# Two-layer hybrid decoder step: the sample recurrence with the state as moving operand, and a rearranged opening

## The chip, the cores and the metric

One NeuronCore of one Trainium2 chip runs one program: two layers of a hybrid decoder. The metric is device time in microseconds (us) of that one execution; every figure below is in microseconds unless it says otherwise.

## What is computed

A layer normalises its input, projects it once to all branches, runs three token mixers and merges them. There are 256 prompt tokens and 8 sample sequences of 8 tokens (64 tokens), 320 tokens in all; the model width is 2048.

```python
h = rms_norm(x, norm_g)
proj = h @ w_in                       # all branch inputs and the merge gates
...
# branch C, gated linear attention, 4 heads, dk 128, dv 256, per sequence:
o = einsum('bhtd,bhde->bhte', qi * exp(b), S)                  # the state read
att = einsum('bhtd,bhsd,bhtsd->bhts', qi, ki, decay)
o = o + einsum('bhts,bhse->bhte', att, vi)
S = exp(b_last)[..., None] * S + einsum('bhsd,bhse->bhde', ki * exp(b_last - b), vi)
...
y = x + merged @ w_out
```

The eight sample sequences start from a state `S` each (4 heads of 128 x 256), and the new states are outputs. The change concerns the line "the state read" for the sample sequences, and the very beginning of the first layer: the scaled input `x * norm_g` and the sum of squares that the norm needs.

## The kernel before, in words

All activations lie transposed: channels on partitions, the 320 tokens along the free axis. Weights stream from HBM in pieces of 128 x 1024 fp32 (512 KB), 298 for each layer. The work on one piece is called a **beat**. For exactness every operand is split into a high part that TensorE takes in its fp32r form and a low part, the rest: ScalarE writes `w_hi` (`split_hi`), VectorE writes `w_lo` (`split_lo`), in two halves of 512 columns, two beats ahead. A beat on TensorE is then 24 matmuls of 128 x 128 weights on 320 tokens (`block_products`: hi x hi, hi x lo, lo x hi), in two halves with a semaphore each.

A layer has 122 beats of input projection, 144 of gates and branch projections and 32 of output projection. Between the beats of the first stretch stand the small matmuls of the mixers, the **side steps**. A hand-written table (`side_steps`, `put(beat, name, k, banks)`) says after which beat each is issued, and which banks of the PSUM tensor `side` it uses. Each engine runs its own program in the order of the beats: in beat b VectorE and ScalarE first split the weights of beat b+2 and then do what the step of beat b hands them (`vector_part`, `scalar_part`). `free_banks` makes TensorE wait until the last reader of a bank has read it.

**The sample recurrence** is eight side steps `sample_gla`, after beats 53, 55, ... 67. Step k takes one head h and one half of the sample sequences (four sequences). For each of two 128-wide pieces of dv it multiplies `att_s` with `v_gla` (64 x 128 weights, 32 columns), and for each of four sequences b a 128 x 128 piece of the sequence's state as weights with eight query columns of `lev_q` (128 x 8), in fp32. The sums stand in bank 3 of `side`, dv on partitions, and after step 7 ScalarE copies all of it into `o_c` (line 1093). Then four fp32r matmuls of 256 columns (`v_stack`, `k_sel`) give the state's increment; VectorE adds it to the decayed state (`sample_state`, line 646) and prepares the next step's `k_sel` (`sample_sel`, line 624). GpSimd's queue (POOL) loads and stores the states, three buffers in turn.

An fp32 matmul of the program stands in the trace as two records; an fp32r one as one.

**The opening** (layer 0, beats 0 to 3): ScalarE's queue issues `params` and the eight pairs of 128-row pieces of x (320 KB each), SyncE's queue (SP) the weight pieces, POOL's queue the constants, masks and the first small weights (2.5 MB). For each pair ScalarE writes `xg_hi` (line 989) and the square of x (line 992), VectorE `xg_lo` (line 415) and two additions to `sq_sum` (lines 419, 423). TensorE needs pairs 0 and 1 and the first weight piece for beat 0, pairs 2 and 3 for beat 1, and so on. After beat 3 it sums `sq_sum` over partitions with one matmul, and ScalarE makes the inverse root of it (`inverse_root`, lines 979, 981, with a table load at line 950). VectorE turns a mask into bytes and clears `q_s` in beat 5 (lines 776, 777); POOL's next loads and two copies from HBM to HBM wait for that.

## Time and profile before

| | us |
|---|---|
| median of 3 runs | 2437.93 (2436.49 to 2440.85) |
| the profiled execution | 2442.46 |
| its span from the first to the last instruction | 2440.7 |
| TensorE (PE) busy | 2382.1, 98% of the span |
| VectorE (DVE) busy | 1374.5, 56% |
| ScalarE (ACT) busy | 1012.4, 41% |
| mean granted TensorE clock | 0.983 of full speed |
| bytes moved | 360.68 MB, 148 GB/s on average |

PE is busy nearly all the time, and the chain of work that ended last lies on it for 87% of the span. So the time is made of what PE is given to do, of the few places where it waits, and of the clock that it is granted. A record of a matmul carries its start and its modelled end; matmuls overlap, so what a matmul costs is read from the distance between starts, not from the duration. The timeline joins neighbouring records of one kind (xN), and gives the start of the first and the length to the end of the last.

### The profile page before, as it was taken

To read this page: it belongs to the slowest core of one execution; us is meant where nothing else is said; L and a number is where in the kernel's file an instruction comes from. 1 tells how busy PE (TensorE), PEld (TensorE's weight loads), DVE (VectorE), ACT (ScalarE), POOL (GpSimd) and SP (SyncE) were. 2 spreads that over 40 slices of the span, in tenths; PEclk is the share of its full clock that TensorE was granted. 3 is DMA by queue.
4 is the path that set the end of the run, shared out by engine and by line. 5 is a ranking of instruction groups with operands and counts; after the bars stand their busy time and mean duration, and the time that the engine had idled before them with its cause. 6 is when DMAs were issued, how large, how long until landed. Compare 5 with 4: busy or idle time off the path is not lost.

```text
span 2440.7 us, 38676 instructions
## 1 busy us (share of the span) xinstructions
PE 2382.1 (98%) x16192; PEld 2334.3 (96%) x16192; DVE 1374.5 (56%) x2324; ACT 1012.4 (41%) x1813; POOL 71.9 (3%) x110
## 2 busy tenths in 40 slices
PE   6999999899999999999999999998999999999998
PEld 6999999799999999999999999998999999999998
DVE  5666656665545455546656675666555455554443
ACT  5335345654333333333342442456443333333332
POOL 0010000000000000000000100000000000000000
PEclk9999999999999999999999998999999999999999
DMA  6333554223444444445553434532244444444453
GB/s 256 113 112 131 187 194 136 90 93 117 152 147 152 151 147 151 152 147 189 195 203 104 147 131 171 189 121 94 80 138 148 153 149 148 153 149 148 153 201 121
DMA packets 97134, 360.68 MB, mean 148 GB/s; under 512 B 11376, under 2 KB 11376, under 8 KB 96128
## 3 DMA queue, kind: packets, MB, share of 16 engines
q1 hardware_dynamic: 85824, 312.51, 38.6%
q0 software_dynamic: 9840, 43.02, 4.8%
q8 instruction: 128, 2.10, 0.4%
q10 hardware_dynamic: 1296, 2.67, 0.3%
q14 instruction: 46, 0.38, 0.1%
HBM read 341.59 MB, written 20.50 MB: 148 GB/s over the span
## 4 chain that ended last, share of the span: by engine, by line
PE 87%; DVE 6%; ACT 3%; issue 2%; DMA 1%; ACTq 0%; POOL 0%; DVEq 0%; POOLq 0%
PE main L1382 79%; PE side L1382 8%; DVE w_lo L380 2%; ACT w_hi L961 1%; ACT probs L1118 1%; PE side L1386 1%; DMA x_first<-in_x_pairs 1%; ACT tc L1158 1%; DVE small L698 0%; DVE probs L693 0%; DVE ta L395 0%; DVE cb L544 0%; DVE probs L721 0%; DVE xg_lo L415 0%; DVE lev_e L558 0%
## 5 line engine op out<-in xcount | busy, mean ns | idle before, releaser
L1382 PE MATMUL main<-xg_hi,w_hi 128*128 128x320 f32 x3488 | 1105.4, 317 | 22.8 <-DVE w_lo L380 20.5
L380 DVE TENSOR_TENSOR w_lo<-raw,w_hi 128x512 fp32r<-128x512 f32 x1192 | 794.3, 700 | 538.7 <-ACT w_hi L961 527.5
L1382 PE MATMUL main<-xg_lo,w_hi 128*128 128x320 f32 x3488 | 1088.1, 312 | 0.0
L1382 PE MATMUL main<-xg_hi,w_lo 128*128 128x320 f32 x3488 | 1087.6, 312 | 0.0
L961 ACT ACTIVATE w_hi<-raw 128x512 fp32r<-128x512 f32 x1192 | 715.8, 627 | 711.3 <-PE main L1382 698.5
L1382 PEld LDWEIGHTS main<-xg_hi,w_hi 128*128 128x128 f32 x3488 | 665.3, 191 | 33.9 <-DVE sq_sum L423 16.7
L1382 PEld LDWEIGHTS main<-xg_lo,w_hi 128*128 128x128 f32 x3488 | 665.3, 191 | 2.0
L1382 PEld LDWEIGHTS main<-xg_hi,w_lo 128*128 128x128 f32 x3488 | 664.2, 190 | 0.0
L1382 PE MATMUL main<-branch_hi,w_hi 128*128 128x320 f32 x768 | 237.3, 309 | 0.0
L1382 PE MATMUL main<-branch_lo,w_hi 128*128 128x320 f32 x768 | 237.3, 309 | 0.0
L1382 PE MATMUL main<-branch_hi,w_lo 128*128 128x320 f32 x768 | 237.3, 309 | 0.0
L1382 PE MATMUL main<-mg_hi,w_hi 128*128 128x320 f32 x512 | 158.2, 309 | 0.0
L1382 PE MATMUL main<-mg_lo,w_hi 128*128 128x320 f32 x512 | 158.2, 309 | 0.0
L1382 PE MATMUL main<-mg_hi,w_lo 128*128 128x320 f32 x512 | 158.2, 309 | 0.0
L1382 PEld LDWEIGHTS main<-branch_hi,w_hi 128*128 128x128 f32 x768 | 144.1, 188 | 0.0
L1382 PEld LDWEIGHTS main<-branch_lo,w_hi 128*128 128x128 f32 x768 | 144.1, 188 | 0.0
L1382 PEld LDWEIGHTS main<-branch_hi,w_lo 128*128 128x128 f32 x768 | 144.1, 188 | 0.0
L1216 ACT ACTIVATE tb<-ta 128x640 f32<-128x640 f32 x48 | 35.6, 742 | 179.8 <-DVE ta L866 179.8
L866 DVE TENSOR_TENSOR ta<-main,rstd 128x640 f32<-128x640 f32 x48 | 39.6, 825 | 103.8 <-PE main L1382 103.8
L1382 PEld LDWEIGHTS main<-mg_hi,w_hi 128*128 128x128 f32 x512 | 96.1, 188 | 0.0
L1382 PEld LDWEIGHTS main<-mg_lo,w_hi 128*128 128x128 f32 x512 | 96.1, 188 | 0.0
L1382 PEld LDWEIGHTS main<-mg_hi,w_lo 128*128 128x128 f32 x512 | 96.1, 188 | 0.0
(218 smaller groups left out, 1459.2 us busy)
## 6 DMA issues: line engine op xcount, KB each, us to landing
raw<-in_w_stream SPq DMA_DIRECT2D x596, 512.0 KB, 3.3
state<-in_state POOLq DMA_DIRECT2D x16, 512.0 KB, 6.2
out_state_s<-state POOLq DMA_DIRECT2D x16, 512.0 KB, 3.0
x_first<-in_x_pairs ACTq DMA_DIRECT2D x8, 320.0 KB, 16.3
w_pool<-in_w_pool POOLq DMA_DIRECT2D x2, 1024.0 KB, 10.7
cache_k<-in_cache_k POOLq DMA_DIRECT2D x2, 1024.0 KB, 5.8
cache_v<-in_cache_v POOLq DMA_DIRECT2D x2, 1024.0 KB, 8.9
out_k_window<-in_cache_k_tok POOLq DMA_DIRECT2D x2, 960.0 KB, 9.9
```

What stands on the lines that cost most here:

```text
L380: dve.tensor_tensor(w_lo[Q % RAWS][:, half], raw[Q % RAWS][:, half], w_hi[Q % HIS][:, half].bitcast(F32), ALU.subtract).then_inc(lo_ready, 1)
L866: dve.tensor_tensor(ta[:, :, :], group_psum(G0), two(rstd[:, :]), ALU.mult).then_inc(main_free, 1)
L961: act.activation(w_hi[Q % HIS][:, half], raw[Q % RAWS][:, half], ACT.Copy).then_inc(hi_ready, 1)
L1118: a(act.activation(p[:, lo:lo + n], p[:, lo:lo + n], ACT.Exp, bias=small[:, 4 + i:5 + i], accum_out=small[:, 12 + i:13 + i]))
L1158: ins = act.activation(tc[32 * q:32 * q + 32, :, :], ta[32 * (q ^ 1):32 * (q ^ 1) + 32, :, :], ACT.Copy)
L1216: give(act.activation(tb[:, :, :], ta[:, :, :], ACT.Sigmoid))
L1382: return pe.matmul(out, lhsT, rhs, start=start, stop=stop)
L1386: return pe.transpose(out, src, ident[0:src.shape[0], 0:src.shape[0]])
```

## The change

Two independent edits stand in one kernel.

**Sample recurrence.** Steps now go half by half (k = 4 * half + head) and not head by head. The state becomes the moving operand: for each of four sequences a matmul with 32 weight columns from the new tile `q_pad` (queries of one head in their own eight columns, zeros beside them) and the 256 columns of the sequence's state. The four write to partitions 0, 32, 64 and 96 of `side` bank 3, and accumulate over the four heads. After the last head of a half ScalarE copies the result, tokens on partitions, to `o_tok`. A new side step `sample_out` (after beat 67, bank 2) adds `att_s` times `v_gla` (8 matmuls of 64 columns) and turns `o_tok` to dv on partitions with a permuted identity (4 matmuls of 128 columns). The steps stand after beats 53, 55, 57, 59, 61, 63, 65, 66. VectorE fills `q_pad` twice in a layer (`sample_queries`, beats 50 and 59).

**Opening.** The odd pairs of x go on SP's queue, between the weight pieces; POOL's loads wait until beat 3 is done. ScalarE loads its table at the start. The squares, 640 columns at a time into `sq_part`, come in beats 1 to 3, after all x has been split; VectorE adds them in whole pairs. The norm's matmul moves from beat 3 to beat 4 (both layers), the first `take` from beat 3 to beat 5, the masks from beat 5 to beat 10.

```diff
+SAMPLE_AT = (53, 55, 57, 59, 61, 63, 65, 66)
...
     for k in range(8):
-        put(53 + 2 * k, "sample_gla", k, (0, 1, 3))
+        put(SAMPLE_AT[k], "sample_gla", k, (0, 1, 3))
+    put(67, "sample_out", 0, (2,))
...
+TAKE[0] = 5
+RMS_BEAT = 4
+def x_at(beat):
+    return {0: (4, 5), 1: (6, 7)}.get(beat, ())
+def squares_at(beat):
+    return {1: (0, 1), 2: (2, 3, 4), 3: (5, 6, 7)}.get(beat, ())
...
             def first_x(j):
-                from_act()
-                sq = (tb, tc)[j % 2]
+                dve.wait_ge(x_hi_ready, j + 1)
...
-                if j == 0:
-                    v(dve.tensor_tensor(sq_sum[:, :], sq[:, 0, :], sq[:, 1, :], ALU.add))
-                else:
-                    for t in range(2):
-                        v.settle()
-                        v(dve.tensor_tensor(sq_sum[:, :], sq_sum[:, :], sq[:, t, :], ALU.add))
+            def first_squares(j):
+                from_act()
+                if j:
+                    tt(sq_part[:, :, :], sq_part[:, :, :], (tb, tc)[j % 2][:, :, :], ALU.add)
                 v.mark("squares_added", 0, j)
+                if j == 7:
+                    tt(sq_sum[:, :], sq_part[:, 0, :], sq_part[:, 1, :], ALU.add)
...
+            def sample_queries(l, half):
+                if half:
+                    wait_step(l, "sample_gla", GH - 1)
+                else:
+                    v(dve.memset(q_pad[:, :], 0.0))
+                    v.settle()
...
+                for h in range(GH):
+                    v(dve.tensor_copy(dst[:, h], src[:, h]))
...
-                if l == 0 and beat == 5:
+                if l == 0 and beat == 10:
                     dve.wait_ge(consts_in, 64)
                     v(dve.tensor_copy(gmask[:, :, :], gmask_f[:, :, :]))
...
-            for j in range(8):
+            for j in (0, 2, 4, 6):
                 act.dma_start(x_first[:, 2 * j:2 * j + 2, :], ins["x_pairs"][j]).then_inc(x_in[j], 16)
+            use_ln_exp()
...
-                    elif name == "sample_gla" and k == 7:
+                    elif name == "sample_gla" and k % GH == GH - 1:
+                        half = k // GH
                         wait_step(l, name, k)
-                        a(act.activation(o_c[:, :, SEQ:TOK], side[:, 3, :].rearrange("p (c n) -> p c n", c=8), ACT.Copy))
+                        a(act.activation(o_tok[:, half, :], side[:, 3, 256 * half:256 * half + 256], ACT.Copy))
+                        a.mark("sample_tok", l, half)
+                    elif name == "sample_out":
+                        wait_step(l, name, k)
+                        a(act.activation(o_c[:, :, SEQ:TOK], side[:, 2, :].rearrange("p (c n) -> p c n", c=8), ACT.Copy))
...
                 sp.dma_start(raw[Q % RAWS][:, :], ins["w_stream"][Q]).then_inc(raw_in[Q % RAWS], 16)
+                if Q < 4:
+                    sp.dma_start(x_first[:, 4 * Q + 2:4 * Q + 4, :], ins["x_pairs"][2 * Q + 1]).then_inc(x_in[2 * Q + 1], 16)
...
+            pool.wait_ge(half_used, last_half(0, 3))
+            load(w_gate[0:RANK, :], ins["w_gate"][0], w_gate_in)
             load(const[:, :], ins["consts"], consts_in)
...
                 elif name == "sample_gla":
-                    h, half = divmod(k, 2)
+                    half, h = half_head(k)
                     pe.wait_ge(state_in[k % STATES], 16 * state_load(l, k))
                     wm("k_sel", l, k)
-                    for t in range(2):
-                        c = 2 * h + t
-                        n = 32 * half
-                        mm(side[:, 3, SMP * c + n:SMP * c + n + 32], v_gla[0:SMP, 2, P * c:P * c + P],
-                           att_s[0:SMP, SMP * h + n:SMP * h + n + 32], True, False)
-                        for b in range(4):
-                            n = 32 * half + TS * b
-                            mm(side[:, 3, SMP * c + n:SMP * c + n + TS], state[:, k % STATES, b, P * t:P * t + P],
-                               lev_q[:, h, SEQ + n:SEQ + n + TS], False, b == 3)
+                    if h == 0:
+                        wm("queries", l, half)
+                    for b in range(4):
+                        mm(side[32 * b:32 * b + 32, 3, 256 * half:256 * half + 256],
+                           q_pad[:, P * h + 32 * b:P * h + 32 * b + 32], state[:, k % STATES, b, :],
+                           h == 0, h == GH - 1)
                     for b in range(4):
                         last = mm(side[:, b // 2, 256 * (b % 2):256 * (b % 2) + 256], k_sel[0:96, b, :],
                                   v_stack[half][0:96, DV * h:DV * h + DV])
+                elif name == "sample_out":
+                    wm("sample_tok", l, 1)
+                    for c in range(8):
+                        pe.matmul(side[:, 2, SMP * c:SMP * c + SMP], v_gla[0:SMP, 2, P * c:P * c + P],
+                                  att_s[0:SMP, SMP * (c // 2):SMP * (c // 2) + SMP], start=c == 0, stop=False,
+                                  skip_group_check=True)
+                    pick = ident.rearrange("p (j h t) -> p h j t", j=4, h=GH)
+                    o4 = side[:, 2, :].rearrange("p (h c n) -> p h c n", h=GH, c=2)
+                    for half in range(2):
+                        for c in range(2):
+                            out = o4[:, :, c, 32 * half:32 * half + 32].rearrange("p h (j t) -> p h j t", j=4)
+                            last = pe.matmul(out, o_tok[:, half, P * c:P * c + P], pick, start=False, stop=True,
+                                             skip_group_check=True)
...
-                    if beat == 3:
+                    if beat == RMS_BEAT:
                         wait_mark(pe, "sq_sum", l, 0)
```

Below is the order of the instructions at three places. The first is the first sample step on TensorE, after the last matmuls of beat 53; `main` is the projection, `side` the step. Before:

```order
L1382 MATMUL main<-xg_hi,w_lo_67 128x320
L1382 MATMUL side<-att_s,v_gla 128x32
L1382 MATMUL side<-lev_q,state 128x8 x4
L1382 MATMUL side<-att_s,v_gla 128x32
L1382 MATMUL side<-lev_q,state 128x8 x4
L1382 MATMUL side<-v_stack_112,k_sel 128x256 x4
L1382 MATMUL main<-xg_hi,w_hi_69 128x320
```

The same place on TensorE in the changed kernel, where `q_pad` gives the 32 weight columns:

```order
L1454 MATMUL main<-xg_lo,w_hi_71 128x320
L1454 MATMUL main<-xg_hi,w_lo_67 128x320
L1454 MATMUL side<-state,q_pad 32x256 x4
L1454 MATMUL side<-v_stack_114,k_sel 128x256 x4
L1454 MATMUL main<-xg_hi,w_hi_69 128x320
```

Ten matmuls with 8 or 32 moving columns have become four with 256; the four of the state's increment are as they were.

The second place is ScalarE's program at the start, with what each row waits for; `tb` and `tc` hold the squares. Before:

```order
L970 DMA par<-in_params 128x98
L972 DMA x_first<-in_x_pairs 128x640 x8
L989 ACT_TABLE_LOAD [waits x_in0,params_in]
L989 ACTIVATE xg_hi<-x_first,par 128x320 [waits vec_done]
L989 ACTIVATE xg_hi<-x_first,par 128x320
L992 ACTIVATE tb<-x_first 128x640
L989 ACTIVATE xg_hi<-x_first,par 128x320 [waits x_in1]
L989 ACTIVATE xg_hi<-x_first,par 128x320
L992 ACTIVATE tc<-x_first 128x640
L961 ACTIVATE w_hi_69<-raw_59 128x512 [waits raw_in0]
```

The same start of ScalarE's program in the changed kernel:

```order
L1024 DMA x_first<-in_x_pairs 128x640 x4
L1002 ACT_TABLE_LOAD
L1040 ACTIVATE xg_hi<-x_first,par 128x320 [waits x_in0,params_in,vec_done]
L1041 ACTIVATE xg_hi<-x_first,par 128x320
L1040 ACTIVATE xg_hi<-x_first,par 128x320 [waits x_in1]
L1041 ACTIVATE xg_hi<-x_first,par 128x320
L1013 ACTIVATE w_hi_69<-raw_59 128x512 [waits raw_in0]
```

The table load no longer stands behind the first x, and the two squares have left the way to the first `w_hi`.

The third place is VectorE's program up to the first `w_lo`, before:

```order
L415 SCALAR_TENSOR_TENSOR xg_lo<-x_first,par,xg_hi 128x320 [waits act_given,params_in,vec_done]
L415 SCALAR_TENSOR_TENSOR xg_lo<-x_first,par,xg_hi 128x320
L419 TENSOR_TENSOR sq_sum<-tb 128x320
L415 SCALAR_TENSOR_TENSOR xg_lo<-x_first,par,xg_hi 128x320 [waits act_given]
L415 SCALAR_TENSOR_TENSOR xg_lo<-x_first,par,xg_hi 128x320
L423 TENSOR_TENSOR sq_sum<-sq_sum,tc 128x320 [waits vec_done] x2
L380 TENSOR_TENSOR w_lo_64<-raw_59,w_hi_69 128x512 [waits hi_ready] x2
```

The same stretch of VectorE's program in the changed kernel:

```order
L448 SCALAR_TENSOR_TENSOR xg_lo<-x_first,par,xg_hi 128x320 [waits x_hi_ready,params_in,vec_done]
L448 SCALAR_TENSOR_TENSOR xg_lo<-x_first,par,xg_hi 128x320
L448 SCALAR_TENSOR_TENSOR xg_lo<-x_first,par,xg_hi 128x320 [waits x_hi_ready]
L448 SCALAR_TENSOR_TENSOR xg_lo<-x_first,par,xg_hi 128x320
L414 TENSOR_TENSOR w_lo_64<-raw_59,w_hi_69 128x512 [waits hi_ready] x2
```

The additions of squares have left, and `xg_lo` waits for `xg_hi` alone.

## Rows read from the trace of the kernel before

**Rows 1.** The page: PE's busy time; the projection's first product, busy and idle.

```profile
PE 2382.1 (98%) x16192; PEld 2334.3 (96%) x16192; DVE 1374.5 (56%) x2324; ACT 1012.4 (41%) x1813; POOL 71.9 (3%) x110
...
L1382 PE MATMUL main<-xg_hi,w_hi 128*128 128x320 f32 x3488 | 1105.4, 317 | 22.8 <-DVE w_lo L380 20.5
```

**Rows 2.** Timeline of PE, first sample step: start, length, instruction, tile, shape.

```profile
263.20 0.31 PE L1382 MATMUL main<-xg_hi,w_lo 128*128 128x320 f32 x1
263.44 0.40 PE L1382 MATMUL side<-att_s,v_gla 64*128 64x32 f32 x2
263.78 1.06 PE L1382 MATMUL side<-lev_q,state 128*128 128x8 f32 x8
...
266.01 0.72 PE L1382 MATMUL side<-v_stack,k_sel 96*128 96x256 f32 x4
266.57 0.31 PE L1382 MATMUL main<-xg_hi,w_hi 128*128 128x320 f32 x1
...
273.71 0.41 PE L1382 MATMUL side<-att_s,v_gla 64*128 64x32 f32 x2
```

**Rows 3.** Stretches: from:to, length, busy (x) by engine, granted clock, DMA share, GB/s.

```profile
294.20:306.00 11.80, 11.80 (x73) 11.50 (x72) 6.62 (x12) 2.48 (x5) 1.06 (x2) 0.86 0.61 215
...
263.40:345.60 82.20, 82.20 (x557) 80.00 (x557) 50.06 (x87) 25.11 (x42) 6.90 (x13) 0.96 0.51 177
1464.00:1550.00 86.00, 86.00 (x563) 83.64 (x562) 49.81 (x87) 24.59 (x41) 6.89 (x13) 0.92 0.48 166
```

**Rows 4.** Timeline of PE, steps whose matmuls write to two partition halves in turn.

```profile
413.51 1.14 PE L1382 MATMUL side<-probs,v_tok 128*64 128x128 f32 x12
414.58 0.41 PE L1382 MATMUL main<-xg_hi,w_hi 128*128 128x320 f32 x1
...
512.19 0.45 PE L1382 MATMUL side<-cache_k,q_s 128*64 128x128 f32 x4
```

**Rows 5.** Timeline of PE, fp32 matmuls of 256 moving columns in the second chunk.

```profile
229.16 1.89 PE L1382 MATMUL side<-v_gla,ko_tok 128*128 128x256 f32 x8
```

**Rows 6.** Timeline of all engines, the opening up to the first matmul.

```profile
1.17 4.27 ACTq L972 DMA_DIRECT2D x_first<-in_x_pairs  x8
...
7.77 1.28 ACT L989 ACT_TABLE_LOAD   x1 [7.77 <-DMA x_first<-in_x_pairs]
...
9.99 0.72 ACT L992 ACTIVATE tb<-x_first 128x640 f32<-128x640 f32 x1
...
11.31 1.02 ACT L989 ACTIVATE xg_hi<-x_first,par 128x320 fp32r<-128x320 f32 x2 [0.61 <-DMA x_first<-in_x_pairs]
...
12.87 1.13 ACT L961 ACTIVATE w_hi<-raw 128x512 fp32r<-128x512 f32 x2
12.99 1.01 DVE L415 SCALAR_TENSOR_TENSOR xg_lo<-x_first,par,xg_hi 128x320 fp32r<-128x320 f32 x2 [0.72 <-ACT tc L992]
...
14.98 1.28 DVE L380 TENSOR_TENSOR w_lo<-raw,w_hi 128x512 fp32r<-128x512 f32 x2
...
15.81 0.61 PE L1382 MATMUL main<-xg_hi,w_hi 128*128 128x320 f32 x1 [15.81 <-DVE w_lo L380]
```

**Rows 7.** Timeline of PE, first matmuls of beats 1 to 3, and the norm's.

```profile
23.03 0.38 PE L1382 MATMUL main<-xg_hi,w_hi 128*128 128x320 f32 x1 [0.73 <-DVE w_lo L380]
...
27.69 0.38 PE L1382 MATMUL main<-xg_hi,w_hi 128*128 128x320 f32 x1 [0.90 <-DVE xg_lo L415]
...
32.84 0.39 PE L1382 MATMUL main<-xg_hi,w_hi 128*128 128x320 f32 x1 [1.41 <-DVE xg_lo L415]
...
36.44 0.70 PE L1382 MATMUL side<-sq_sum,ones 128*128 128x320 f32 x2
```

**Rows 8.** DMA of the first 22 us: all packets, and POOL's queue (q0).

```profile
DMA packets 2559, 7.79 MB, mean 354 GB/s; under 512 B 447, under 2 KB 447, under 8 KB 2431
...
q0 software_dynamic: 544, 2.49, 28.1%
```

**Rows 9.** Timeline of DVE in beat 10, waiting for the gate step.

```profile
64.17 1.93 DVE L534 TENSOR_SCALAR lev_q<-side,par 128x320 f32<-128x320 f32 x4 [3.35 <-PE side L1382]
```

More of the change, by code:

```diff
@@ L258, in trunk @@
         probs = [probs0, probs1]
+        q_pad = place("q_pad", [P, GH * (P + TS)], at=probs0_at)
         main = ctx.enter_context(nc.psum_tensor("main", [P, 4, 512], F32))
@@ L766, in vector_part @@
             def vector_part(l, beat):
-                if l == 0 and beat < 2:
-                    for j in range(4 + 2 * beat, 6 + 2 * beat):
-                        first_x(j)
-                if l == 0 and beat == 1:
-                    v.settle()
-                    v.mark("sq_sum", 0, 0)
-                if l == 0 and beat == 5:
+                if l == 0:
+                    for j in squares_at(beat):
+                        first_squares(j)
+                if l == 0 and beat == 10:
                     dve.wait_ge(consts_in, 64)
@@ L848, in vector_part @@
                 for k in range(8):
-                    if beat == 51 + 2 * k:
+                    if beat == (SAMPLE_AT[k - 1] if k else 51):
                         sample_sel(l, k)
+                if beat in (50, SAMPLE_AT[GH - 1]):
+                    sample_queries(l, int(beat != 50))
                 if beat in (68, 70):
@@ L917, in _ @@
                         split_lo(1)
+                    if l == 0:
+                        for j in x_at(beat):
+                            first_x(j)
                     vector_probs(l, beat)
@@ L1040, in scalar_part @@
             def scalar_part(l, beat):
-                if l == 0 and beat < 2:
-                    for j in range(4 + 2 * beat, 6 + 2 * beat):
-                        first_x(j)
-                if beat == 3:
+                if l == 0:
+                    for j in squares_at(beat):
+                        first_squares(j)
+                if beat == RMS_BEAT:
                     act.wait_ge(rms_done, l + 1)
@@ L1227, in _ @@
                         split_hi(1)
+                    if l == 0:
+                        for j in x_at(beat):
+                            first_x(j)
                     split_hi(Q + 2)
@@ L1294, in _ @@
                 for k in range(STATES):
-                    load(state[:, k, :, :], ins["state"][l, k], state_in[k])
+                    load(state[:, k, :, :], ins["state"][l, state_no(k)], state_in[k])
                 s, n = marks[("hist", l, 3)]
```

45 lines of the change are left out of this document (32 added, 13 removed).

## The prediction

> **What bounds the kernel now.** I read the page first: TensorE (PE) is busy 98% of the span, and the projection's largest group waited only 22.8 us in all, of which 20.5 on `w_lo` [rows 1]. So there are three things to gain from: matmul time, the few waits, and the clock. The timeline of PE then gives the prices, always from start to start. A projection matmul takes 0.147: the last of beat 53 starts at 263.20, so the next would start at 263.35. The next projection matmul starts at 266.57 [rows 2]; a sample step therefore costs 3.22, sixteen times, 51.5. The next step starts 10.27 later: 24 matmuls at 0.147 are 3.52, and two such beats and one step make 10.26, so PE has no wait here.
>
> The clock comes next. The stretch of one such period from 294.20 to 306.00 lasts 11.80 and not 10.27, at a mean granted clock of 0.86 [rows 3]; TensorE has two levels, 1.2 and 2.4 GHz, and it fell to the lower one right behind a step. Over the whole phase the mean is 0.96 in layer 0 and 0.92 in layer 1 [rows 3]. Time times the missing share is 3.3 and 6.9; with 1.53 for each spoilt period, two in layer 0, it is 3.1, and so I take 3.1 and 6.1, together 9.2.
>
> The opening: the first matmul starts at 15.81 [rows 6]; beats 1, 2 and 3 then begin with waits of 0.73, 0.90 and 1.41, and the norm's matmul comes at 36.44 [rows 7].
>
> **The sample step.** Removed are two `att_s` matmuls and eight of the state with eight columns: everything from 263.35 to 266.01, 2.66, most of it paid for loading 128 weight columns for eight moving ones (eight records in 1.06, or 0.115 each) [rows 2]. Added are four fp32 matmuls of 256 columns. Such a matmul is two records of 0.216: eight records take 1.89 including a last duration of about 0.38 [rows 5]. One after the other the four would take 1.73. Side by side, each in its own 32 columns of the array, they would take 0.43. What does the trace say of that? In the attention step with two halves of 64 columns, twelve records of 128 columns, half as many as in [rows 5] and so 0.108 each, take 1.07 from the first start to the next projection matmul at 414.58 [rows 4]; in a row they would be 1.30, in perfect parallel 0.65. Four records at 512.19 end within 0.45, less than the 0.60 of a row of four at 0.108 with a last duration of 0.27 [rows 4]. So two column tiles do overlap, with a loss of 0.2 to 0.42 at the seams. Four tiles at a time no row shows. The bounds are 0.43 and 1.73 plus the change of tile shape, 0.09 on each side (a first side matmul comes 0.24 behind the projection and not 0.147 [rows 2]). I take full overlap with a loss of 0.3: 0.09 + 0.43 + 0.30, and the unchanged four `k_sel` matmuls, 0.12 each, 0.48 [rows 2]. That is **1.30 a step**, a gain of 1.92, sixteen times **30.7**. The lower bound (no loss but the tile change) is 1.09 (34.1), the serial one 2.39 (13.3).
>
> The Trainium skill speaks against the overlap, in "TensorE: Matmul & The Clock Gate", Part 3 (Packing small matmuls): a weight load passes an in-flight matmul only when its row group differs, and column tiles share the row groups. By that rule the four would come one after the other; the two-half steps of this trace do not agree. The same part gives 2.38 times for three column tiles, which would put the four, as an estimate with the same efficiency for each tile, near 0.55 and the sum 2.9 lower.
>
> **The new step `sample_out`.** Eight fp32 matmuls of 64 columns with 64 x 128 weights are sixteen records at 0.115 to 0.13 (like the `att_s` pair, 0.40 less one duration of 0.27, and the eight-column row) [rows 2]: 1.84 to 2.1. Four of 128 columns are eight records at 0.115: 0.92. With the changes of shape this is 3.0, twice: **6.0** added. It waits for ScalarE's copy of step 7's output, a PSUM read of 256 columns. Beat 67, 3.52, lies between, and ScalarE's queue holds nothing else there but a copy for the gate; I cost the wait at nothing, and at 1 if the cover is gone.
>
> **Waits in the shorter phase.** Two beats and a step now last 8.34 and not 10.27. VectorE is busy 50.06 of 82.20 [rows 3]; the same work in 66 is three quarters, with the splits still two beats ahead. I place its work in a period: take, state, `k_sel`, two splits, two products, and each `w_lo` is ready 3 or more before PE wants it. `k_sel` for step 7 is the tightest, as steps 6 and 7 are now one beat apart: VectorE needs about 0.3 + 1.7 + 0.7 behind step 6, against 3.52. The state for step 7 is loaded behind step 5, which leaves some 11 for a store issue, a load issue and a landing. The fills of `q_pad` (a memset and four small copies) stand on VectorE's queue behind the pooling's work; queued behind them is a `w_lo` two beats ahead. Nothing for all of this, up to 1 if one is late.
>
> **The clock.** Removed are the long stretches of almost empty matmuls behind which it fell. I give back all **9.2**; none is the other bound, and then the new `sample_out` (2 us of narrow matmuls, where a step had 2.7) is where it would fall.
>
> **The opening.** DMA moved 7.79 MB in the first 22 us, of it 2.49 by POOL's queue [rows 8]. Without those and with two queues for x, I expect pair 0 at 6.4 (it was 7.77) and pair 1 at 6.2 (it was 11.31) [rows 6]. The table load of 1.28, which stood behind pair 0, is under the wait. From there: two pairs of `xg_hi` at 1.02, a `w_hi` piece of 1.13; VectorE's `xg_lo` at 1.01 a pair ends at 9.5 and the first half of `w_lo` (half of 1.28) at 10.1 [rows 6]. So PE starts at **10.1**, 5.7 earlier; the squares (0.72 each) and additions that stood between are moved. Bounds are 9.3 and 12: x slower than I count.
>
> Do beats 1 to 3 still wait? On ScalarE each beat needs 2.04 of `xg_hi` and 1.13 of `w_hi`, 3.2; on VectorE 2.02 and 1.28, 3.3, below 3.52, and PE's first beat gives time as well: before it took from 15.81 to 22.30 (23.03 less its wait), 2.97 over the 3.52, at the lower clock (its first record is 0.61 long, later ones 0.31 [rows 2, 6, 7]). I take 2.5 for that after. x and the first five weight pieces are the 5.3 MB that are left of the 7.79 [rows 8]; at the same 0.4 MB/us they are in by 16.5, pair 7, just ahead of the last piece, at 15.2. Counting both engines on from there, its `xg_lo` ends at 19.3, and PE wants it at 23.1 (10.1 + 3 x 3.52 + 2.5). So the three waits, 3.0, go too. PE is through beat 3 at 26.7 (10.1 + 14.1 + 2.5) against 36.44: **9.7**. What is late next is the norm: squares of pairs 5 to 7 end on ScalarE near 27, their additions on VectorE near 28.5, and PE asks after beat 4, at 30.1. Masks in beat 10 (1.6) fall into VectorE's 3.35 of waiting for the gate step [rows 9]. Constants are issued at 27 and wanted at about 50. The HBM copies now run in beats 11 and 12 and delay weight pieces there, which are a beat or more ahead.
>
> **Sum.** 30.7 - 6.0 + 9.2 + 9.7 = 43.6. From the profiled execution's 2442.46 (span 2440.7 and 1.8 around it) this gives 2398.9; that execution stands 4.5 above the median of the runs, 2437.93, from which it gives 2394.3. The runs differ by how often the clock falls, which the 9.2 was read from at the high end. I forecast the middle, **2396**; the rivals are counted from the same middle, 2440.2.
>
> **Rivals.**
> Tiles in a row: the four matmuls don't overlap, by the rule named above or another. A step is 2.39, the gain 13.3 and not 30.7, and the clock may still fall behind it (half of 9.2): 2440.2 - 13.3 + 6.0 - 4.6 - 9.7, about 2419. For it: no row with four tiles. Against: [rows 4]. 0.12.
> Two at a time: the moving operands of four tiles can't all be read at once. Four records' time, 0.86, and the loss: a step of 1.73, gain 23.8: 2403. 0.15.
> The clock falls elsewhere: steps and opening as forecast, but low stretches stand behind `sample_out` or in the attention, whose waits now fall otherwise: 2405. 0.10.
> Slower than before: a wide moving operand of fp32 state in a 32-column tile runs at a quarter of its rate, in a row. The four then take 6.9, a step 7.6; sixteen times 4.3 is 69, less 9.7 and plus 6.0: about 2505. It decides from a step of 3.5 on, where 16 times the excess over 3.22 eats the opening's net 3.7. For it: no row moves fp32 through so narrow a tile. Against it: the `v_tok` step keeps its rate in tiles of 64 columns [rows 4]. 0.02.
> The opening does not do what it says: x is no earlier because weights and x share the bandwidth, and only the table load and squares (1.28 + 1.44) are saved: 2403. 0.06, else as forecast.
>
> **How the numbers follow.** The forecast has 0.55, from 2387 (from the median, with the lower bound of the step, 3.4, the opening at 9.3, 0.8, and 3 for a luckier clock) to 2402 (the step's loss at 0.42, PE's start at 12, one late item). With two at a time, the clock and the opening's rival 0.86 lies between 2387 and 2409 (2406 and 3 for the clock); the serial and the slower case are left out. The range is **2385 to 2410**. A change of 0.2%, about 5 us, is what a measurement of this kernel can tell from none: faster 0.96, same 0.01, slower 0.03.
>
> **What would show it.** In the timeline after: the first projection matmul near 10.1, no wait before beats 1 to 3, the norm's matmul near 30. Sample steps of four `state` matmuls whose records start together in fours, 1.3 between the projection's matmuls, and a clock of 1.00 over the phase. One `sample_out` of 3.0 in each layer with no wait before it. The layer's remaining time unchanged. A distance of 0.216 between all eight records, or a wait of PE on `k_sel`, `sample_tok` or `sq_sum`, would make me wrong.

## The result, and the profile after

The changed kernel takes **2395.23** (median of 4 runs, 2394.26 to 2398.78), the kernel before 2438.35 beside it (4 runs, 2436.49 to 2440.85). The ratio is 0.9825, with a 95% interval of 0.9808 to 0.9842: faster by 1.75%. The forecast was 2396, with a range of 2385 to 2410.

The profiled execution took 2395.89 (before 2442.46), so the two traces explain a difference of 46.6. The page of the changed kernel, with span, busy times by engine and the projection's first product (busy, mean ns, idle before and its releaser), answers to [rows 1]:

```profile
span 2394.1 us, 38415 instructions
PE 2345.3 (98%) x16048; PEld 2293.9 (96%) x16048; DVE 1374.9 (57%) x2335; ACT 1010.8 (42%) x1816; POOL 71.7 (3%) x110
...
L1454 PE MATMUL main<-xg_hi,w_hi 128*128 128x320 f32 x3488 | 1102.5, 316 | 12.8 <-DVE w_lo L414 12.8
```

PE is busy 36.8 less and waits 10.0 less before this group: 46.8 together. (How long PE is busy depends on the clock too, so this is no count of work.) The other engines do what they did.

**The step.** Timeline of PE and of its weight loads (PEld) at the first sample step, which answers to [rows 2]:

```profile
253.53 0.31 PE L1454 MATMUL main<-xg_hi,w_lo 128*128 128x320 f32 x1
253.77 0.16 PEld L1454 LDWEIGHTS side<-state,q_pad 128*32 128x32 f32 x8 [0.19 <-issue]
253.77 0.64 PE L1454 MATMUL side<-state,q_pad 128*32 128x256 f32 x8
254.34 0.75 PE L1454 MATMUL side<-v_stack,k_sel 96*128 96x256 f32 x4
254.92 0.31 PE L1454 MATMUL main<-xg_hi,w_hi 128*128 128x320 f32 x1
```

The projection would have gone on at 253.68 (253.53 and 0.147) and goes on at 254.92: a step costs 1.24, where it cost 3.22. The four fp32 matmuls of 256 columns (eight records) take 0.57 up to the next start. In the records' own nanoseconds, four start 7 ns apart and the other four 0.22 later. So the first records of the four matmuls run side by side, then the second ones: all four column tiles work at once. The four `k_sel` matmuls take 0.58.

**The new step**, from the timeline of PE after beat 67:

```profile
312.78 0.31 PE L1454 MATMUL main<-xg_hi,w_lo 128*128 128x320 f32 x1
313.02 2.00 PE L1565 MATMUL side<-att_s,v_gla 64*128 64x64 f32 x16
314.95 1.16 PE L1573 MATMUL side<-const,o_tok 128*128 128x128 f32 x8
315.86 0.40 PE L1454 MATMUL main<-xg_hi,w_hi 128*128 128x320 f32 x1
```

It costs 2.93 (from 312.93 to 315.86) and there is no wait ahead of it. The clock over the stretch of the steps, in both layers (columns as in [rows 3]):

```profile
250.00:340.00 90.00, 89.91 (x634) 83.54 (x633) 64.14 (x115) 38.04 (x63) 7.92 (x15) 1.00 0.62 221
1460.00:1550.00 90.00, 89.90 (x622) 85.10 (x621) 57.44 (x99) 43.45 (x71) 7.30 (x13) 1.00 0.61 211
```

**The opening.** The timeline of PE, ScalarE and VectorE; of PE, these are all rows up to beat 5 that carry a wait or belong to the norm:

```profile
3.39 1.28 ACT L1002 ACT_TABLE_LOAD   x1 [3.39 <-issue]
6.24 0.56 ACT L1040 ACTIVATE xg_hi<-x_first,par 128x320 fp32r<-128x320 f32 x1 [1.57 <-DMA x_first<-in_x_pairs]
...
9.26 1.28 DVE L414 TENSOR_TENSOR w_lo<-raw,w_hi 128x512 fp32r<-128x512 f32 x2
...
10.09 0.61 PE L1454 MATMUL main<-xg_hi,w_hi 128*128 128x320 f32 x1 [10.09 <-DVE w_lo L414]
...
28.10 0.49 DVE L429 TENSOR_TENSOR sq_sum<-sq_part 128x320 f32<-128x320 f32 x1
...
30.30 0.70 PE L1454 MATMUL side<-sq_sum,ones 128*128 128x320 f32 x2
```

PE starts at 10.09 and not 15.81 [rows 6], and the three waits of [rows 7] are gone. The norm's operand is ready at 28.59, 1.7 before PE asks.

**Where the time went.** The 596 beats can be cut at the moments at which a beat's last matmul ends. Two stretches of each layer changed. The table gives the lengths in the profiled execution of four kernels (`e1_opening` has the opening's edits alone, `e2_sample` the sample recurrence's alone); the sample steps lie in beats 50 to 71.

| | before | after | e1_opening | e2_sample |
|---|---|---|---|---|
| layer 0, start to the end of beat 3 | 36.60 | 26.93 | 26.24 | 36.48 |
| layer 0, beats 4 to 49 | 210.67 | 210.66 | 209.30 | 209.39 |
| layer 0, beats 50 to 71 | 109.55 | 93.66 | 106.49 | 93.66 |
| layer 0, beats 72 to 121 | 247.80 | 247.57 | 247.72 | 247.39 |
| layer 1, beats 4 to 49 | 211.02 | 209.38 | 210.62 | 209.33 |
| layer 1, beats 50 to 71 | 112.66 | 93.66 | 106.49 | 93.66 |
| layer 1, beats 72 to 121 | 247.54 | 247.40 | 247.44 | 247.72 |
| beats 122 to 297 of each layer | 619.52 | 619.52 | 619.52 | 619.52 |

From before to after: 9.67 in the opening, 15.89 and 19.00 in the sample steps' beats, 2.0 elsewhere, where nothing was changed. Every later comparison reads from such lengths.

How far does such a length repeat? Five other kernels below have the opening of the kernel after unchanged (`e1_opening`, `e3_one_tile`, `e4_two_tiles`, `e8_narrow_pad`, `e9_wide_pad`). Their first matmul starts between 9.93 and 10.28, but their beat 3 ends between 25.66 and 26.46, and in the kernel after at 26.93. In all six, beats 1 to 3 last 3.52 each without a wait; what differs is beat 0, 5.08 to 5.62 in the five and 6.29 in the kernel after, by how many of its 24 matmuls ran before the clock rose (starts 0.27 apart, and 0.15 behind that). So differences of one microsecond at beat 3 can't be put down to an edit by one pair of traces.

### The profile page after: what moved, and what is told of

Read it like the earlier page. It is cut to its first block, busy times and chain, and to the rows that moved or that the text cites. A ratio compares the mean times of both kernels' runs of the same rounds, so it can differ in the third digit from the quotient of the medians.

```text
span 2394.1 us, 38415 instructions
## 1 busy us (share of the span) xinstructions
PE 2345.3 (98%) x16048; PEld 2293.9 (96%) x16048; DVE 1374.9 (57%) x2335; ACT 1010.8 (42%) x1816; POOL 71.7 (3%) x110
## 4 chain that ended last, share of the span: by engine, by line
PE 89%; DVE 6%; ACT 3%; issue 2%; DMA 0%; POOL 0%; DVEq 0%; ACTq 0%; POOLq 0%
PE main L1454 81%; PE side L1454 7%; DVE w_lo L414 2%; PE side L1458 1%; ACT probs L1180 1%; ACT w_hi L1013 1%; ACT tc L1220 0%; DVE small L748 0%; DVE lev_e L594 0%; DVE cb L580 0%; DVE probs L743 0%; DVE probs L771 0%; DMA x_first<-in_x_pairs 0%; DVE ta L429 0%; DVE probs L770 0%
## 5 line engine op out<-in xcount | busy, mean ns | idle before, releaser
L1454 PEld LDWEIGHTS main<-xg_hi,w_hi 128*128 128x128 f32 x3488 | 663.0, 190 | 22.5 <-DVE xg_lo L448 10.1
```

Of the source, the lines that this page charges most:

```text
L1454: return pe.matmul(out, lhsT, rhs, start=start, stop=stop)
```

## The experiments

All are told as changes of the kernel after, and each was timed beside the kernel before; the theory and the rival of each run stand in what was expected of it.

**The two parts alone.** `e1_opening` has the old sample steps, `e2_sample` the old opening. Their cores, against the kernel after:

```diff
-    put(67, "sample_out", 0, (2,))
-                        mm(side[32 * b:32 * b + 32, 3, 256 * half:256 * half + 256],
-                           q_pad[:, P * h + 32 * b:P * h + 32 * b + 32], state[:, k % STATES, b, :],
+                            mm(side[:, 3, SMP * c + n:SMP * c + n + TS], state[:, k % STATES, b, P * t:P * t + P],
+                               lev_q[:, h, SEQ + n:SEQ + n + TS], False, b == 3)
```

```diff
-            for j in (0, 2, 4, 6):
+            for j in range(8):
...
-            pool.wait_ge(half_used, last_half(0, 3))
...
-                    if beat == RMS_BEAT:
+                    if beat == 3:
```

> The opening's edits alone, with the sample recurrence as before. Theory (the two parts add, each as the changed kernel's trace shows it): beat 3 ends 9.7 us earlier (26.9 and not 36.6), nothing behind it changes, so 2438.4 - 9.7 = 2428.7. The low clock stays behind the sample steps, at about 0.96 and 0.92 in the two phases. Rival (the opening's gain was partly the shorter sample phase meeting another clock): more than 2431 or less than 2426.

> The sample recurrence's edits alone, with the opening as before. Theory: 16 steps at 1.25 and not 3.23 save 31.7, sample_out costs 2 x 3.0, and the low clock of the two phases (9.2 us in the profiled run) is gone because its cause, long stretches of narrow matmuls, is gone: 2438.4 - 34.9 = 2403.5. Rival (the clock fell less in the changed kernel only because the opening shifted everything in time): 2438.4 - 25.7 = 2412.7, with clock below 1.00 in the phases.

Measured: e1_opening 2423.78 (6 runs, 2420.94 to 2428.80) beside 2434.29, ratio 0.9959 (0.9945 to 0.9973), so 10.5 gained, by the interval 6.6 to 13.4; e2_sample 2404.89 (4 runs) beside the same, ratio 0.9885 (0.9867 to 0.9903), so 29.4, by the interval 23.6 to 32.4. Its expected 34.9 lies outside and the rival's 25.7 inside, but the rival's reason, a clock that still falls in the sample beats, is not what its trace shows: they last 93.66 in both layers, as in the kernel after. What was too high is the loss that the kernel before was charged with, as the next rows show. The parts add up to 39.9. The 43.1 of the whole change was measured beside other runs of the kernel before, with a median of 2438.35 and not 2434.29; the difference of 3.2 is less than that between the two medians. What did not come as expected is the clock in e1_opening. Its stretches with the old steps, in both layers:

```profile
243.00:350.00 107.00, 106.90 (x729) 102.72 (x728) 66.83 (x119) 39.16 (x62) 7.94 (x15) 1.00 0.55 194
1458.00:1565.00 107.00, 106.90 (x735) 103.64 (x734) 65.66 (x111) 43.52 (x70) 9.43 (x17) 1.00 0.56 196
```

The clock was 1.00 throughout, behind the very steps behind which it had fallen to 0.96 and 0.92 [rows 3]. Two things follow. First, the old phase at full clock is 106.49 long, so the profiled kernel before lost 3.06 and 6.17 to the clock there: 9.2, as the prediction read. Second, this loss is not paid by every execution. The other runs tell how much varies: 22 further runs of the kernel before lie between 2430.38 with a mean clock of 0.987 and 2441.99 with 0.983, and those of e1_opening between 2420.94 with 0.988 and 2428.80 with 0.984. The profiled execution of the kernel before, 2442.46, was slower than all of these.

**How many tiles work at once.** `e3_one_tile` gives the four matmuls the same 32 partitions, `e4_two_tiles` two places in turn. The columns streamed are the same; the sums in `side` are then not the state read.

```diff
-                        mm(side[32 * b:32 * b + 32, 3, 256 * half:256 * half + 256],
+                        mm(side[0:32, 3, 256 * half:256 * half + 256],
```

```diff
-                        mm(side[32 * b:32 * b + 32, 3, 256 * half:256 * half + 256],
+                        mm(side[32 * (b % 2):32 * (b % 2) + 32, 3, 256 * half:256 * half + 256],
```

> The changed kernel, but the four state matmuls of a step all write to the first 32 partitions, so they use one column tile (the sample tokens' recurrent output is therefore wrong, the work is the same in number and shape). Theory (the gain rests on four tiles running at once): their eight records follow one another at 0.216, 1.73 and not 0.48, so a step costs 2.5, 16 x 1.25 = 20 more: about 2415. Rival (the gain comes from the swap of operands alone, and the four are hidden or overlapped anyway): 2395 to 2398.

> The changed kernel, but the four state matmuls of a step use two column tiles in turn (output wrong as in the run with one tile). Theory (each tile streams at its own full rate): records come in pairs at 0.216, 0.87 in all, so a step costs 0.4 more, 16 x 0.4 = 6.4: about 2401.6. Rival (already two tiles lose at the seams, as the two-half attention steps did, 0.3 a step): about 2406.

Timeline of PE and PEld at one step of e3_one_tile, then of e4_two_tiles:

```profile
270.36 0.31 PE L1454 MATMUL main<-xg_hi,w_lo 128*128 128x320 f32 x1
270.60 1.91 PE L1454 MATMUL side<-state,q_pad 128*32 128x256 f32 x8
270.60 1.43 PEld L1454 LDWEIGHTS side<-state,q_pad 128*32 128x32 f32 x8 [0.19 <-issue]
272.44 0.74 PE L1454 MATMUL side<-v_stack,k_sel 96*128 96x256 f32 x4
273.02 0.31 PE L1454 MATMUL main<-xg_hi,w_hi 128*128 128x320 f32 x1
```

```profile
268.11 0.31 PE L1454 MATMUL main<-xg_hi,w_lo 128*128 128x320 f32 x1
268.35 1.06 PE L1454 MATMUL side<-state,q_pad 128*32 128x256 f32 x8
268.35 0.57 PEld L1454 LDWEIGHTS side<-state,q_pad 128*32 128x32 f32 x8 [0.19 <-issue]
269.34 0.74 PE L1454 MATMUL side<-v_stack,k_sel 96*128 96x256 f32 x4
269.92 0.31 PE L1454 MATMUL main<-xg_hi,w_hi 128*128 128x320 f32 x1
```

To the next start the four matmuls take 1.84 in one tile, 0.99 in two, 0.57 in four; a step 2.51, 1.66, 1.24. The sample beats are 103.85 and 96.97 long in each layer, against 93.66: 1.27 and 0.41 more a step. The whole kernels take 2414.48 (2 runs, 2413.80 to 2415.15) and 2400.60 (2 runs, 2399.40 to 2401.79). The prediction gave its first two rivals 2.39 and 1.73 a step, near these, so the runs would have told them apart, and neither is what the kernel does.

**What the opening is made of.** Three runs take one part of it back each: POOL's loads at the start again (`e5_pool_early`); all of x on ScalarE's queue (`e6_one_queue`); the squares right behind each pair's `xg_hi` and `xg_lo` (`e7_squares_inline`).

```diff
-            pool.wait_ge(half_used, last_half(0, 3))
```

```diff
-            for j in (0, 2, 4, 6):
+            for j in range(8):
...
-                if Q < 4:
-                    sp.dma_start(x_first[:, 4 * Q + 2:4 * Q + 4, :], ins["x_pairs"][2 * Q + 1]).then_inc(x_in[2 * Q + 1], 16)
```

```diff
-    return {1: (0, 1), 2: (2, 3, 4), 3: (5, 6, 7)}.get(beat, ())
+    return ()
...
                         first_x(0)
+                        first_squares(0)
```

> The changed kernel, but POOL's loads (2.5 MB) are issued at the start again. Theory (the DMA bandwidth of about 0.4 MB/us is the limit on when x is in): the last pair lands near 21.5 and not 15.4, PE starts a little later, near 11, and beats 2 and 3 wait for xg_lo; beat 3 ends near 29.5 and not 26.9, +2.5 us in all: 2398. Rival (the arrival of x does not matter once two queues carry it): beat 3 ends at 27, 2395.

> The changed kernel, but all eight pairs of x go on ScalarE's queue. Theory: pair 1 lands near 8 and not 5.8, the first matmul comes 1.1 later, at 11.2, and the later beats don't wait: +1.1, 2396.3. Rival (the weight pieces of SP take half the bandwidth, so the last pairs come too late): waits before beats 2 and 3, +3 or more.

> The changed kernel, but each pair's square and its addition stand right behind the pair's split again. Theory: ScalarE's two squares (0.65 each) put the first matmul at 11.4, and VectorE's load for each beat, 2.0 + 1.3 + 1.6 = 4.9, is over the beat's 3.52, so beats 2 and 3 wait; beat 3 ends near 30.6 and not 26.9: +3.7, 2399. Rival (VectorE and ScalarE have the time beside PE's first beat at the low clock): beat 3 ends by 28.3, +1.3.

| | first matmul | length of beat 0 | end of beat 3 | time |
|---|---|---|---|---|
| after | 10.09 | 6.29 | 26.93 | 2395.23 |
| e5_pool_early | 10.37 | 6.35 | 29.17 | 2400.00 (2 runs) |
| e6_one_queue | 11.78 | 5.26 | 27.59 | 2395.84 (2 runs) |
| e7_squares_inline | 11.58 | 5.64 | 30.18 | 2400.27 (2 runs) |

Waits of PE behind its first matmul, of e5_pool_early up to beat 5 and then of e7_squares_inline up to beat 3:

```profile
21.90 0.39 PE L1453 MATMUL main<-xg_hi,w_hi 128*128 128x320 f32 x1 [1.66 <-DVE w_lo L414]
...
34.33 0.81 PE L1453 MATMUL side<-sq_sum,ones 128*128 128x320 f32 x2 [1.63 <-DVE sq_sum L429]
```

```profile
21.13 0.38 PE L1464 MATMUL main<-xg_hi,w_hi 128*128 128x320 f32 x1 [0.39 <-DVE w_lo L414]
26.43 0.39 PE L1464 MATMUL main<-xg_hi,w_hi 128*128 128x320 f32 x1 [1.54 <-DVE w_lo L414]
```

Holding back POOL's loads saves 2.2 up to beat 3, nearly all of it the wait in beat 2, and, which the expectation left out, another 1.6 at the norm: the late pairs make the squares late too. In e5_pool_early beat 2's weight piece has landed at 16.6, in the kernel after at 12.4. The squares' move saves 3.25: PE starts 1.5 earlier, and the waits in beats 2 and 3 go. The second queue lets PE start 1.7 earlier. In this pair of traces 0.7 of it is left at beat 3, but not because something else held beats 1 to 3: they last 3.52 each in both kernels. Beat 0 lasts 6.29 with the early start and 5.26 with the late one, as more of it ran at the low clock. Against the five other traces with the opening of the kernel after (beat 3 through at 25.66 to 26.46) e6_one_queue is 1.1 to 1.9 later. By these traces, of which one has a single queue, the second queue is worth 0.7 to 1.9 at beat 3. In the time of the whole kernel e6_one_queue can't be told from the kernel after. No run takes back the early table load alone, so its share of the 5.7 is not measured.

**Which work the clock falls behind.** Two kernels put some 3.5 us of useless work into each of the sixteen new steps: 16 fp32 matmuls of 8 columns with 128 weight columns, as the old step had them (`e8_narrow_pad`), or 24 fp32r matmuls of 320 columns, as the projection has them (`e9_wide_pad`).

```diff
+                    for n in range(16):
+                        mm(side[:, 2, 8 * n:8 * n + 8], state[:, k % STATES, n % 4, 0:P],
+                           lev_q[:, h, SEQ:SEQ + TS])
```

```diff
+                    for n in range(24):
+                        mm(side[:, 2, 0:TOK], xg_hi[:, n % KT_D, 0:P], xg_hi[:, n % KT_D, :])
```

> The changed kernel with sixteen more fp32 matmuls of eight moving columns in each sample step, written to an unused part of a bank (32 records at 0.112, 3.6 us more a step). Theory (long stretches of narrow matmuls bring the clock down behind them): 16 x 3.6 = 57.6 more and the low clock behind many of the steps, 1.5 us or more each time, together 16 to 40: 2470 to 2490, granted clock clearly under 1.00 in the sample phase. Rival (where the clock falls has nothing to do with narrow matmuls): 2453, clock 1.00 there.

> The changed kernel with 24 more fp32r matmuls of 320 moving columns in each sample step (3.53 us more a step, as much time as the narrow ones of the other padded run). Theory (it is the emptiness of narrow matmuls that lowers the clock, not a longer pause of the projection): 16 x 3.53 = 56.4 more and nothing else, 2451.7, clock 1.00 in the sample phase. Rival (any longer step does it): 2465 or more.

The stretches of the sample beats in layer 0, e8_narrow_pad first, then e9_wide_pad:

```profile
253.90:386.80 132.90, 132.80 (x911) 127.11 (x911) 67.92 (x118) 42.99 (x71) 9.33 (x17) 0.91 0.46 155
```

```profile
245.10:366.90 121.80, 121.70 (x845) 114.78 (x844) 67.90 (x123) 40.91 (x65) 7.93 (x15) 1.00 0.48 166
```

The wide work costs 28.11 in eight steps, 3.51 each, which is 24 times 0.147: nothing but itself. The narrow work by itself should cost 3.6 a step, 32 records at 0.112, and 28.8 in eight; it cost 39.3. The 10.5 more are the clock, 0.91 against 1.00. The first five periods of two beats and a step are alike, 13.39 long and not 11.9; the sixth is at full clock again, 11.85, and the rest is lost in the last beats. In layer 1 the first six periods are 13.39. The first three:

```profile
265.13 0.64 PE L1454 MATMUL side<-state,q_pad 128*32 128x256 f32 x8
265.70 3.74 PE L1454 MATMUL side<-lev_q,state 128*128 128x8 f32 x32
...
278.52 0.64 PE L1454 MATMUL side<-state,q_pad 128*32 128x256 f32 x8
...
291.91 0.64 PE L1454 MATMUL side<-state,q_pad 128*32 128x256 f32 x8
```

The times of the whole kernels are 2472.61 (2 runs; ratio 1.0145, 1.0101 to 1.0189) and 2448.64 (3 runs; ratio 1.0053, 1.0034 to 1.0072). So it is this narrow work and not busy time ahead of the projection that takes the clock away, as the prediction assumed when it gave the clock back. The trace counts both kinds as busy. The two kinds differ in their type too, fp32 against fp32r, which this pair doesn't separate; against the type speaks that fp32 matmuls of 128 columns alone brought the clock up in `e10_warm_early` below, and that `e3_one_tile`, with 1.84 of fp32 matmuls of 256 columns in each step, lost nothing to the clock in its sample beats (103.85 in both layers, which is 8 times 1.27 over the kernel after).

**Can more be had?** `e10_warm_early` runs useless fp32 matmuls from 1.09 on so that beat 0 finds the full clock, splits the first weight piece ahead of x, and lets PE wait for odd pairs only in the second half of a beat. `e11_fill` has these edits and adds wide useless matmuls before three attention steps (`p_turn`), where PE waits and the clock falls; its own edit stands second.

```diff
+            for _ in range(18):
+                mm(side[:, 0, 0:P], ones[:, :], ones[:, :])
...
+                        split_hi(0)
                         first_x(0)
                         first_x(1)
-                        split_hi(0)
```

```diff
+                    for n in range({3: 18, 4: 5, 6: 11}.get(k, 0)):
+                        mm(side[:, banks[0], 0:TOK], xg_hi[:, n % KT_D, 0:P], xg_hi[:, n % KT_D, :])
                     wm("probs", l, k)
```

> The changed kernel with three edits in the opening: the first weight piece is split before x is touched, the second half of each of the first beats alone waits for the second pair of x, and TensorE runs 18 fp32 matmuls of ones, without use, from the start until about 8 us. Theory: the first useful matmul comes at 8.3 and not 10.1, and beat 0 takes 3.6 and not 6.3 as the clock is already up; then ScalarE's and VectorE's 3.3 a beat and the landing of x bound beats 1 to 3, so beat 3 ends near 23.1 and not 26.9, and the norm's matmul then waits about 1 for the squares: 3 us less than the changed kernel, 2392.2. Rival (the splits bound it as before): beat 3 ends at 25.5 or later, less than 1.5 gained.

> The run before with useless wide matmuls also in the attention: 18, 5 and 11 fp32r matmuls of 320 columns in front of three steps of each layer where TensorE waits 2.84, 0.96 and 1.83 for VectorE. Theory: they fill the waits and keep the clock up behind them (10 us at the low level in each layer in the changed kernel's profile), 3 to 4 us for each layer: about 2385. Rival (the low clock comes from the narrow matmuls around, not from the waits, and the fillers end after the waits would have): 2392 or more.

Measured: 2394.74 (4 runs, 2393.68 to 2397.74; ratio 0.9832, 0.9814 to 0.9850) and 2395.43 (5 runs, 2392.26 to 2396.18; ratio 0.9827, 0.9810 to 0.9845): neither can be told from the kernel after, where 2392.2 and about 2385 were expected. The waits of PE in e10_warm_early up to beat 15:

```profile
8.53 0.42 PE L1454 MATMUL main<-xg_hi,w_hi 128*128 128x320 f32 x1 [1.43 <-DVE xg_lo L448]
13.40 0.38 PE L1454 MATMUL main<-xg_hi,w_hi 128*128 128x320 f32 x1 [1.09 <-DVE w_lo L414]
28.85 0.81 PE L1454 MATMUL side<-sq_sum,ones 128*128 128x320 f32 x2 [1.14 <-DVE sq_sum L429]
69.64 0.64 PE L1454 MATMUL main<-xg_hi,w_hi 128*128 128x320 f32 x1 [1.97 <-DVE w_lo L414]
```

The first part did what it was meant to: beat 0 starts 1.6 earlier and at full clock, and beat 3 ends at 24.18, 2.75 earlier. Then PE asks for the norm before it is ready (1.14 of waiting, 1.4 with what follows it), and behind the wait at 69.64, which the kernel after has too, PE fell to the low clock (first record 0.64 long). That beat lasts 7.27 here and 7.28 in e11_fill, which has the same opening, and 5.75 or less in every other trace: the early opening met a low clock there both times. Beats 4 to 49 are 1.6 longer than in the kernel after, those of layer 1 1.4, that layer's attention 1.7, and 1.85 slower is what this profiled execution is. At the end of beat 49 the two kernels with the early opening stand at 236.45 and 236.08, the five others with the opening of the kernel after at 234.78 to 235.78, and the profiled kernel after itself, slow in its beat 0 and in beats 22 to 26 (told below), at 237.60. What was gained by beat 3 is lost. In e11_fill the clock of the attention is better, yet its beats 72 to 121 last 247.31 and 247.36 against 247.57 and 247.40. Timeline of PE, the fillers and the waits of the attention in layer 0 of e11_fill, then the same steps in the kernel after:

```profile
435.24 2.80 PE L1454 MATMUL side<-xg_hi 128*128 128x320 f32 x18
438.16 0.87 PE L1458 MATMUL side<-const,probs 128*128 128x128 f32 x6
...
448.94 0.90 PE L1454 MATMUL side<-xg_hi 128*128 128x320 f32 x5
452.06 0.88 PE L1458 MATMUL side<-const,probs 128*128 128x128 f32 x6 [2.23 <-DVE probs L771]
```

```profile
439.75 1.51 PE L1458 MATMUL side<-const,probs 128*128 128x128 f32 x6 [2.84 <-DVE probs L771]
...
453.65 0.84 PE L1458 MATMUL side<-const,probs 128*128 128x128 f32 x6 [0.96 <-DVE probs L771]
```

The first fillers cover the wait of 2.84 and the low clock behind it is gone. But the next operand comes from VectorE, and comes no sooner: the two steps are 13.90 apart in both kernels (438.16 to 452.06, 439.75 to 453.65). What the clock gives back becomes filler and wait. A low clock ahead of a wait is thus hidden by it in beats 96 to 98. Beat 102 is different: it lasts 7.25 with fillers and 8.79 without, a gain of 1.54. But beats 107 to 113, which e11_fill leaves as they were, then take 1.32 more. Two of these beats in the kernel after, 107 and 113, columns as before:

```profile
502.50:511.43 8.93, 8.93 (x58) 8.27 (x59) 5.47 (x10) 3.67 (x6) 0.00 (x0) 0.81 0.18 59
543.27:550.67 7.40, 7.40 (x59) 6.75 (x59) 2.50 (x4) 1.64 (x3) 0.00 (x0) 1.00 0.23 73
```

PE is busy throughout both, so no wait hides this loss of 1.5. Beats 107, 109 and 111 of the kernel after have it in layer 0 (8.93, 8.93, 8.92), and every trace has a loss of this kind in at least two of the four beats 107 to 113. Whether it can be had back was not tried.

## Why the prediction was right

The mechanisms were right; that the totals agree so closely is in part luck. The measured 43.1 against 43.6 rests on four runs of the kernel before with a median of 2438.35. The 22 later ones, in three groups, have medians of 2434.29, 2435.67 and 2435.56, from which the kernel after is 39.1 to 40.4 lower. And the clock term of 9.2, read from a slow execution, was taken whole, where the medians of the runs show some 3.6.

- **The step.** 1.30 forecast, 1.24 measured; sixteen times 1.98 is 31.7 against 30.7. Inside, the seam loss was too high (of its range of 0.2 to 0.42 only the upper end, 1.07 less 0.65, comes out of [rows 4]) and `k_sel` too low: the four state matmuls take 0.57 where 0.43 and 0.30 were summed, the `k_sel` matmuls with the return to the projection 0.58 and not 0.48. The sum counted the change of shape, 0.09, once, its two bounds counted it twice; counted twice it would have been 1.39, and the 0.58 shows where the second one lies. The two-half steps of [rows 4] had the right answer to the question on which most chance hung, whether column tiles overlap. The rule quoted from the Trainium skill ("TensorE: Matmul & The Clock Gate", Part 3) is not what happens here: all eight weight loads are recorded within 0.16 while matmuls on the same rows are in flight, and within 1.43 when they share one tile. Its figure for three tiles, 2.38 times, which the prediction carried over to an estimate of 0.55, stands beside a measured 0.57.
- **`sample_out`.** 3.0 forecast, 2.93 measured, no wait ahead of it; twice 5.9.
- **The clock.** 9.2 forecast, and 9.2 is what the profiled pair shows (3.06 and 6.17). This term was right for that execution and too high for the median: e2_sample gained 29.4 against a clean 25.8 (31.7 less 5.9), so 3.6, and by its interval (23.6 to 32.4) anything from nothing to 6.6. The prediction allowed for it by taking the middle between the profiled execution and the median; one trace alone can't tell that another execution pays nothing here. (Its two values have their middle at 2396.6.)
- **The opening.** PE at 10.09 (10.1 forecast), no waits before beats 1 to 3, beat 3 through at 26.93 (26.7), so 9.67 (9.7). The squares were summed at 28.59 (28.5), the norm asked for at 30.30 (30.1). For the first beat 2.5 over 3.52 was taken; it was 2.77 in this execution and 1.56 to 2.10 in five others, so the 26.7 was met by a slow beat 0. The early start is made as told, by the second queue (1.7) and the squares' move (1.5), and what frees beats 1 to 3 is the squares' move and POOL's delay. The prediction gave POOL's delay no value at the norm, where it is 1.6 more.
- **Elsewhere.** By the table 44.6 of the 46.6 lie in the opening and the steps' beats. The other 2.0 lie in beats 4 to 49 of layer 1 (1.64) and in the attention (0.4), where only waits and clock differ: the prediction expected these stretches unchanged. Of the 1.64, 1.4 is a difference of clock in beats 22 to 26. Those five beats in layer 1 of the kernel before, and in layers 0 and 1 of the kernel after:

```profile
1310.01:1342.08 32.07, 29.33 (x200) 28.64 (x201) 21.25 (x29) 9.23 (x17) 3.50 (x3) 0.89 0.25 83
```

```profile
98.46:130.45 31.99, 29.22 (x200) 28.61 (x201) 21.25 (x29) 9.33 (x17) 3.50 (x3) 0.89 0.26 83
1283.94:1314.65 30.71, 27.79 (x201) 27.09 (x201) 21.27 (x29) 9.22 (x17) 3.52 (x3) 0.94 0.26 86
```

The kernel after has the longer form in one layer and the shorter in the other. Over the 13 traces the stretch is 30.4 to 30.8 long or 31.9 to 32.1, the longer form 8 times in 26, under either opening and either kind of step. So these 1.4 of the 46.6 are not shown to be the change's; they are a difference between executions.
- **The rivals.** Serial and two at a time were priced right, as e3_one_tile and e4_two_tiles show, and did not happen. The clock did not fall behind `sample_out`. Of a narrow tile running at a quarter of its rate there is no sign: in `e3_one_tile`, where they follow one another, a record of 256 columns in a 32-column tile takes about 0.22, as in [rows 5].

## What to carry to other kernels

When many small matmuls have full weights and a few moving columns, count the matmuls and not the columns: a record with 128 weight columns cost 0.11 to 0.12 here with 8, 64 or 128 moving columns (that the weight load is the reason, as the prediction has it, no run separates). Turning the operands round, with the small one as 32-column weights in four column tiles, cut this step from 3.22 to 1.24, although it streams 16 times the columns of the state read it replaces. Read a kernel's clock losses from several executions before giving them back in a sum, and where the clock should stay, look at what the busy time is made of: 3.5 of wide work a step cost nothing more, 3.6 of narrow work took the clock. In an opening, follow the chain past the first matmul: of 1.7 of earlier start between 0.7 and 1.9 was left three beats later, depending on when the clock rose, and 2.75 gained by beat 3 met the next late operand and a low clock. And look at how a length varies among traces in which it should be the same before a microsecond of it is put down to an edit.

## What the hardware showed that was not expected

- Four column tiles of 32 with 128 rows and fp32 operands work side by side: 1.84, 0.99 and 0.57 for the same four matmuls in one, two and four tiles, each with a change of shape in it, which costs about 0.09.
- The low clock is a matter of the single execution. The same sixteen steps lost 9.2 in one and nothing in another, and whole runs of the kernel before, which differ by 11.6, follow their mean clock by and large (0.988 to 0.983).
- Making the narrow stretch longer turned the occasional loss into one of nearly every period, in the one trace there is of it: 13.39 in the first five periods of layer 0 and the first six of layer 1, 1.5 over their own work, which is about what a spoilt period of the old step lost [rows 3].
